# A two-block float32 model on one core: in the hybrid mixers, value products half a slot later, Exp and Ln from one table set, softplus sum and causal mask in other places

## The reference, cut to what matters

```python
proj = h @ w_in
q, k, v, z, xbc, dt = jnp.split(proj, [Q_END, K_END, V_END, Z_END, XBC_END], axis=-1)
...
attn = dilated_attention(q, k, v)
xbc = jax.nn.silu(causal_depthwise_conv(xbc, conv_w, conv_b))
...
dt = jax.nn.softplus(dt.astype(jnp.float32) + dt_bias.astype(jnp.float32))
a_neg = -jnp.exp(a_log.astype(jnp.float32))
y = ssd_chunked(xs, dt, a_neg, bm, cm) + d_skip[:, None] * xs
y = rmsnorm(y * jax.nn.silu(z), ssm_norm)
return jnp.concatenate([attn, y], axis=-1) @ w_out
```

## Time and profile before

| what | value |
|---|---|
| time, three runs | 2692.08, 2696.5 and 2701.61 us, median 2696.5 us |
| span of the profiled execution, first to last instruction | 2693.9 us |
| PE busy | 2601.8 us, 97% of the span |
| DVE, ACT, POOL busy | 1815.6, 1467.9 and 173.1 us |
| mean granted TensorE clock | 0.993 of full speed |

### The profile page before, as it was taken

The page is one execution under the profiler, slowest core; times in us unless marked ns, Lnnn a source line. Parts: engine busy times, 40 slices in busy tenths (PEclk is TensorE's granted clock), DMA queues, the critical chain, the costliest instruction groups (busy, mean ns, idle before and its releaser), DMA issues.

```text
span 2693.9 us, 44003 instructions
## 1 busy us (share of the span) xinstructions
PE 2601.8 (97%) x15456; PEld 2255.8 (84%) x15456; DVE 1815.6 (67%) x2565; ACT 1467.9 (54%) x2363; POOL 173.1 (6%) x253
## 2 busy tenths in 40 slices
PE   7999998999999989999989999999999999998999
PEld 6888887888888868888888688888888888887887
DVE  5766668666766666676676666676657667666766
ACT  4645447455555564565555655555555555555654
POOL 0010001000000030000001200000110000002000
PEclk9999999999999999999999999999999999999999
DMA  4458744477566436666654266666446665653664
GB/s 150 145 164 231 210 129 142 156 226 212 172 193 190 133 121 208 191 184 193 187 176 153 70 199 191 177 192 191 141 149 183 196 202 168 192 157 121 180 189 146
DMA packets 581774, 465.44 MB, mean 173 GB/s; under 512 B 19524, under 2 KB 542372, under 8 KB 581156
## 3 DMA queue, kind: packets, MB, share of 16 engines
q1 hardware_dynamic: 579300, 456.10, 56.3%
q0 software_dynamic: 1632, 7.37, 1.1%
q10 hardware_dynamic: 736, 0.56, 0.1%
HBM read 460.76 MB, written 4.25 MB: 173 GB/s over the span
## 4 chain that ended last, share of the span: by engine, by line
PE 83%; DVE 7%; ACT 5%; issue 2%; DVEq 2%; DMA 1%; POOL 1%; SPq 0%; ACTq 0%; POOLq 0%
PE acc L783 19%; PE gu L750 14%; PE tp L750 13%; PE tp L757 7%; PE gu L757 7%; PE acc L816 3%; DVE lo_a L452 3%; ACT hi_a L440 1%; PE acc L1454 1%; PE acc L1456 1%; PE acc L1455 1%; PE gu L701 1%; PE gu L1412 1%; PE tp L1327 1%; PE gu L1413 1%
## 5 line engine op out<-in xcount | busy, mean ns | idle before, releaser
L452 DVE TENSOR_TENSOR lo_a<-raw_a,hi_a 128x2048 fp32r<-128x2048 f32 (+1 forms) x313 | 711.1, 2272 | 357.4 <-ACT hi_a L440 356.1
L440 ACT ACTIVATE hi_a<-raw_a 128x2048 fp32r<-128x2048 f32 (+1 forms) x313 | 591.5, 1890 | 119.0 <-PE acc L1456 27.4
L750 PE MATMUL tp<-xT,hi_a 128*128 128x512 f32 x1600 | 398.4, 391 | 0.0
L750 PE MATMUL gu<-xT,hi_a 128*128 128x512 f32 x1600 | 397.9, 391 | 0.0
L750 PEld LDWEIGHTS gu<-xT,hi_a 128*128 128x128 f32 x1600 | 294.0, 188 | 56.9
L750 PEld LDWEIGHTS tp<-xT,hi_a 128*128 128x128 f32 x1600 | 293.4, 188 | 56.4
L783 PE MATMUL acc<-hi_b,h_hi 128*128 128x512 f32 x760 | 298.6, 393 | 1.6 <-issue 1.1
L783 PE MATMUL acc<-lo_b,h_hi 128*128 128x512 f32 x760 | 298.0, 392 | 0.0
L783 PE MATMUL acc<-hi_b,h_lo 128*128 128x512 f32 x760 | 295.7, 389 | 0.0
L464 DVE TENSOR_TENSOR lo_b<-raw_b,hi_b 128x1024 fp32r<-128x1024 f32 x210 | 255.9, 1219 | 0.0
L842 ACT ACTIVATE arena<-arena 128x256 f32<-128x256 f32 x200 | 83.6, 418 | 282.0 <-DVE arena L905 282.0
(11 more groups left out here) (329 smaller groups left out, 4109.4 us busy)
## 6 DMA issues: line engine op xcount, KB each, us to landing
raw_a<-in_ffn_w_in SPq DMA_DIRECT2D x352, 512.0 KB, 5.7
raw_b<-in_ffn_w_out SPq DMA_DIRECT2D x176, 512.0 KB, 3.6
raw_a<-in_w_in SPq DMA_DIRECT2D x52, 512.0 KB, 4.7
raw_a<-in_w_gate SPq DMA_DIRECT2D x44, 512.0 KB, 5.5
raw_a<-in_w_up SPq DMA_DIRECT2D x44, 512.0 KB, 6.7
raw_b<-in_w_down SPq DMA_DIRECT2D x44, 512.0 KB, 4.4
raw_a<-in_w_out SPq DMA_DIRECT2D x24, 512.0 KB, 4.2
raw_a<-in_c_w_in SPq DMA_DIRECT2D x24, 512.0 KB, 4.5
```

The lines of the kernel that those rows point to most:

```text
L440: nc.scalar.activation(a_view(hi_a, par)[:, :, 0:width], a_view(raw_a, par)[:, :, 0:width], ACT.Copy).then_inc(a_hi, 1)
L452: nc.vector.tensor_tensor(a_view(lo_a, par)[:, :, 0:width], a_view(raw_a, par)[:, :, 0:width], a_view(hi_a, par)[:, :, 0:width].bitcast(F3 ...
L750: nc.tensor.matmul(banks[:, e, :], w_hi[:, kt, e * P:(e + 1) * P], xT[:, :, kt, :], start=(kt == 0), stop=False)
```

## The change

It is made in the hybrid stages alone. The value products of a unit are made at p + 4 in place of p + 3, ahead of the scores that are made at the same place, and go to bank 2 of `acc` in place of the part of `tp`. So turning a unit no longer waits for the unit before to be read out; in its stead the value products of unit w wait until those of unit w - 1 have been read out (the first until `cs_out`, as bank 2 holds the cumulative sums before that). ScalarE copies the high part at p + 4, after the next slot's high weights; VectorE takes the rest at p + 5.

On ScalarE a table set that has Exp and Ln is loaded at p = 9, ahead of the copies of dt. The four groups of exponentials under the causal mask are taken two at p = 17, one at the end of p = 18 and one at p = 19 ahead of the Silus. On VectorE the end of softplus goes ahead of the low weights at p = 11, and the causal mask is added at the end of p = 15 and 17.

```diff
+        def values_bank(s):
+            return acc[:, 2, 0:256] if s.kind == "hybrid" else tp[:, 1, 256:512]
 # woven_turn_pe
-            elif w >= 1:
+            elif w >= 1 and s.kind != "hybrid":
                 pe.wait_ge(o_lo, s.pair0 + w)
 # woven_values_pe
             pe.wait_ge(pt_act, g + 1)
+            if s.kind == "hybrid":
+                pe.wait_ge(*((o_lo, s.pair0 + w) if w else (cs_out, s.layer + 1)))
...
-                        mm = nc.tensor.matmul(tp[r, 1, 256 + t * P:512], v[:, t, c:c + HD], probs_t[:, cols_t],
+                        mm = nc.tensor.matmul(values_bank(s)[r, t * P:256], v[:, t, c:c + HD], probs_t[:, cols_t],
 # middle_pe
-            if scored(s, p - 3) is not None and s.kind != "B":
-                woven_values_pe(pe, s, scored(s, p - 3))
+            behind = p - (4 if s.kind == "hybrid" else 3)
+            if scored(s, behind) is not None and s.kind != "B":
+                woven_values_pe(pe, s, scored(s, behind))
 # bc_pe
-            pe.wait_ge(cs_out, L + 1)
             pe.wait_ge(row_out, L + 1)
             pe.wait_ge(soft_ready, s.unit0 + 4)
+            pe.wait_ge(o_lo, s.pair0 + 4)
 # hybrid_act
                     if p == 9:
+                        nc.scalar.preload_act_table_set("natural_log_exp_and_others")
                         narrow_evac_act(act, s, 3, dt_out)
...
-                    if scored(s, p - 3) is not None:
-                        values_act(act, s, scored(s, p - 3))
...
-                    if 15 <= p < 19:
-                        decay_act(act, s, (p - 15) // 2, 2 * ((p - 15) % 2))
+                    if p == 17:
+                        decay_act(act, s, 0, 0)
+                        decay_act(act, s, 0, 2)
+                    if p == 19:
+                        decay_act(act, s, 1, 2)
                     if p == 19:
                         for k in range(4):
                             silu_act(act, s, k)
...
                     if h == 0:
                         ahead_a(hi_slot_a, act, s.a0 + i + 1)
+                    if scored(s, p - 4) is not None:
+                        values_act(act, s, scored(s, p - 4))
+                    if p == 18:
+                        decay_act(act, s, 1, 0)
 # hybrid_dve
+                    if p == 11:
+                        softplus_sum_dve(dve, s)
                     if h == 1:
                         ahead_a(lo_slot_a, dve, s.a0 + i + 1)
...
-                    if p in (10, 11):
-                        (softplus_ratio_dve, softplus_sum_dve)[p - 10](dve, s)
+                    if p == 10:
+                        softplus_ratio_dve(dve, s)
...
-                    if scored(s, p - 3) is not None:
-                        values_dve(dve, s, scored(s, p - 3))
+                    if scored(s, p - 5) is not None:
+                        values_dve(dve, s, scored(s, p - 5))
...
-                    if p in (14, 16):
-                        causal_dve(dve, s, (p - 14) // 2)
+                    if p in (15, 17):
+                        causal_dve(dve, s, (p - 15) // 2)
```

More of the change, by code:

```diff
@@ L1506, in values_act @@
             act.wait_ge(o_ready, s.pair0 + u + 1)
-            nc.scalar.activation(oT_hi[:, u, :], tp[:, 1, 256:512], ACT.Copy).then_inc(o_hi, 1)
+            nc.scalar.activation(oT_hi[:, u, :], values_bank(s), ACT.Copy).then_inc(o_hi, 1)
         def exp_act(act, s, w):
@@ L1548, in values_dve @@
             dve.wait_ge(o_hi, s.pair0 + u + 1)
-            nc.vector.tensor_tensor(oT_lo[:, u, :], tp[:, 1, 256:512], oT_hi[:, u, :].bitcast(F32),
+            nc.vector.tensor_tensor(oT_lo[:, u, :], values_bank(s), oT_hi[:, u, :].bitcast(F32),
                                     ALU.subtract).then_inc(o_lo, 1)
```

## The result

The changed kernel takes 2702.63 us (median of 20 runs, 2698.23 to 2704.17), the kernel before 2696.47 (20 runs, 2692.08 to 2703.55). The ratio is 1.0016 with an interval of 1.0009 to 1.0022, so 2.4 to 5.9 us slower; the medians differ by 6.2, the means by 4.8, as six of the twenty times of the kernel before lie above 2700. That is inside the 0.3% (8.1 us) that the prediction counted as no change, on its slow side. The forecast was 2699.6, 3.1 slower: inside the interval, half of what the medians show. The profiled execution took 2702.65 with a span of 2700.8: 1.85 lie around a span, not the 2.6 that I had carried over. The spans differ by 6.9.

What follows compares the result with a forecast made beforehand. TensorE is busy almost throughout, so only its gaps can be won. Each hybrid stage was to be 1.5 us slower, 3.1 for both: span 2697.0, with about 2.6 around it 2699.6; range 2690 to 2707.

Steps and rivals of the forecast that it cites:

- the sums: First hybrid: cumulative sums start 2.4 us earlier, after one TensorE wait of 2.85 in place of 1.85 and 2.04.
- the half clock behind that wait: TensorE after the wait: sums 1.3 us, then twelve products at half clock, 2.67, ending at 70.5.
- my upper bound: Unit 2's scores reach VectorE at 73.3 us if TensorE's clock is half through both groups.
- the 2.1 that I carried on: Unit 2's scores reach VectorE at 72.2 us, before at 74.29, so 2.1 earlier.
- The bound for full clock: Unit 2's scores reach VectorE at 71.7 us if the clock stays full; `cs_out` then holds the values.
- what follows: Unit 3's scores at 81.45 us, evacuation at 91.7, `bc_pe` at 112.0 after a TensorE wait of 3.0.
- the rival: Half clock behind the waits ahead of the sums and at `bc_pe`: 2.0 to 5.2 us slower per hybrid; chance 0.18.
- My 7.2: From `bc_pe` at 112.0 us, through VectorE's taps and low weights, to slot 11's low products at 119.2.
- the hold on the mask: VectorE's mask, started while GpSimd multiplies by the reciprocals, is held 0.6 us; bounds 0 to 1.65.
- the table set: ScalarE's earlier Ln and next Exp, without their loads of 1.28 us, cost and give nothing on the path.
- the first (faster): Second Silu comes early enough that `bc_pe` waits for nothing: 2.3 us faster per hybrid, 2691.8; chance 0.15.
- the second, the clock: Waits ahead of the sums and at `bc_pe` each bring half clock: slower, about 2705 us; chance 0.18.

Runs made afterwards that it cites:

- the second trace: The changed kernel, unaltered, profiled once more; 2700.76 us, one execution.
- run 7: Changed kernel with softplus sum at p = 10, copy of cumulative sums at p = 11, and mask at p = 16 and 18; 2688.51 us, ratio 0.9969.
- run 4: Changed kernel without the load of one table set for Exp and Ln; 2704.21 us, ratio 1.0022.
- Run 5: Changed kernel with twenty useless TensorE products ahead of each of two waits, for the softplus sum and the second Silu; 2700.31 us, ratio 1.0015.

## Why the prediction was right in direction and too small

**Right: the sums.** 13.33 against 13.3, after one wait of 2.63 against 2.85.

**Wrong: the price of the half clock behind that wait** ("I take half ... 70.5", twelve products only). From the sums' start to unit 2's scores on VectorE I had 5.7; the trace has 73.38 - 65.78 = 7.6. The sums themselves took 2.36 (65.78 to 68.14) where I had 1.3, the products 2.86 against 2.67, the values 1.41 against 0.8. It is 0.8 beyond my upper bound, since that still had the sums at full clock. In the second trace, at full clock, the same way takes 5.9: it is `cs_out` that then holds the values, 1.10. The bound for full clock had that, but as 5.2, with `cs_out` 1.1 behind the low weights; in that trace it comes 1.8 behind them (67.91 to 69.73), with the evacuation of a slot (0.66) between. So of the 2.1 that I carried on, 0.14 or 1.87 was there, by the execution.

**Right: what follows.** Unit 2's to unit 3's scores took 9.45 in either trace (forecast 9.25), the evacuation 9.98 behind those (10.25), `bc_pe` 20.55 behind that (20.3), where it waited 2.78 (3.0). From there to slot 11's low products 7.5 (7.2), in the second trace 8.0: half clock behind `bc_pe`, which only the rival had. My 7.2 was VectorE's taps and low weights; the row at 120.83 shows no wait for these, so there TensorE itself sets the time. (Two of the four Silus take 1.1, not the 2.1 of my sum; its 110.3 is right.)

**Too dear: the hold on the mask.** It took 2.62 against 2.28 undisturbed, 0.34 in place of 0.6; GpSimd paid instead, 3.66 in place of 1.61. The Trainium skill, "SBUF — State Buffer", section "SBUF: two separate sides", has the one that starts first keep the ports for its instruction. GpSimd started first (90.13), the mask next, and GpSimd's second instruction ended last: the order of the rows agrees with that rule, the hold of 0.34 being short for one of GpSimd's two instructions (1.61 for both). In run 7 it is the mask that pays: it starts 0.74 after GpSimd and takes 3.02, GpSimd 1.61. TensorE's wait of 0.85 for it (line 1313), which I had at nothing, ended well ahead of `bc_pe`.

**Right: the table set**, by run 4. Of the rivals, the first (faster) is refuted by the wait of 2.78; the second, the clock, is the missing size: the forecast plus what half clock took beyond it at the sums (1.9) is 3.4 for a hybrid, and the first trace has 3.9. Run 5 puts a number on it: with the clock at 1.00 the steps of the first hybrid are the forecast's to 0.5 (19.22, 28.67, 38.65, 59.20, 66.44), and the time is 2700.31, 0.7 above the forecast; the other 2.3 by the medians go with the half clock. That the forecast comes so near at full clock is in part luck: its 0.5 of half clock stands where `cs_out` took 0.7 more than I had.

What I did not see is how the parts divide. I argued one chain in which the sum wins and `bc_pe` takes back; the runs show one good edit, worth 5.4 by the medians, and two that cost as much each. The later values move unit 0's values from a place where TensorE waited anyway to between the sums and unit 2's scores, and add their wait for `cs_out`. The later mask moves the first group of exponentials out of ScalarE's idle time; run 7 wins the time back by making that idle time shorter (3.33 in place of 5.87). Open is what decides after which wait the clock falls.

## What to carry over

Here work that stood in front of a wait was free, and the same work behind it was on the path, with a new wait of its own: before moving an instruction half a slot, look at what the engine does in both places, and at what its new bank waits for. When an edit joins two waits into one, give its bound the half clock from the first instruction behind the wait, and read two traces of the same kernel before pricing it. Test the parts of a combined change singly: here the one part that gains was hidden by two that lose.

## What was not expected of the hardware

- The same wait of 2.6 was followed by 1.2 GHz in one trace of a kernel and by 2.4 GHz in the next. The spans differ by only 1.8 us (2700.8 and 2699.0): in the second trace the low stretch came at the other wait.
- Twenty products with no use in each of two waits kept the granted clock at 1.00 through both stages (0.94 to 0.96 without them); by the medians that was worth 2.3 of the 6.2 us.
- A table load of 1.28 was followed by the next activation 1.29 after its start (59.27 and 60.56 in run 4, 110.86 and 112.15 after the change), with nothing more to pay.
